# Delta rule: the inverse's first five levels on packed 32x32 diagonal blocks, the sixth as one off-diagonal block product

## The chip, the cores and the metric

The program runs on one core of one Trainium2 chip. The time is the device time of one execution in microseconds; the number given for a kernel is the median of its runs. The engines are named as in the profile: PE (TensorE, its weight loads apart as PEld), DVE (VectorE), ACT (ScalarE), POOL (GpSimd), SP (SyncE).

## What is computed

The whole program is a two-layer attention block followed by a second block with a gated delta rule and a Fourier mixer (512 positions, 256 of context, width 1024, 4 heads). The change touches one step of the second block, the inverse of a unit triangular matrix for each chunk of 64 positions, head and direction:

```python
CHUNK = 64
    lower = jnp.tril(jnp.ones((CHUNK, CHUNK), dtype=bool))
    strict = jnp.tril(jnp.ones((CHUNK, CHUNK), dtype=bool), -1)
...
    a_mat = jnp.where(strict, jnp.einsum('nbhid,nbhjd->nbhij', kb, kc) * decay, 0.0)
    eye = jnp.eye(CHUNK, dtype=f32)
    t_inv = lax.linalg.triangular_solve(eye + a_mat, jnp.broadcast_to(eye, a_mat.shape),
                                        left_side=True, lower=True, unit_diagonal=True)
    u_val = jnp.einsum('nbhij,nbhjd->nbhid', t_inv, vb)
    w_key = jnp.einsum('nbhij,nbhjd->nbhid', t_inv, kb * jnp.exp(gc)[..., None])
...
    def step(s, xs):
        u_i, w_i, a_i, qd_i, kd_i, gl_i = xs
        v_new = u_i - jnp.einsum('bhcd,bhde->bhce', w_i, s)
        o_i = jnp.einsum('bhcd,bhde->bhce', qd_i, s) + jnp.einsum('bhij,bhje->bhie', a_i, v_new)
        s = s * jnp.exp(gl_i)[..., None, None] + jnp.einsum('bhcd,bhce->bhde', kd_i, v_new)
```

Both directions are run: 12 chunks, 4 heads, 2 directions, 96 inverses of 64x64.

## The kernel before

The program is written out by hand, engine by engine: each engine has its own list of instructions and waits on semaphores, and nothing but those lists sets the order. Nearly all of the time PE multiplies 128x512 tiles of weights (the helper lines L977 to L979). The delta rule is a stretch of some 130 us late in the program.

The 96 inverses are made in three **groups** `g` (0, 1, 2). A group holds, for each direction `d`, two tiles of 128 positions (`j`), four heads (`h`) and the two chunks of a tile (`c`, partitions 0 to 63 and 64 to 127). One direction of a group is so one tile of 128 partitions x 512 columns, eight blocks of 64 columns, with two 64x64 matrices above each other in each. The inverse grows by doubling in six **levels**: at level `lev` the diagonal blocks of size 2^lev are known, and pairs of them are joined:

- POOL `mask` (L3562) writes `a_level`, the part of `a_mat` that couples the pairs.
- PE `level_z` (L1575) multiplies it by `tt_mat`, the inverse so far, transposed: 16 matmuls of 64x64 by 64x64 for a direction, those of `c` = 0 on one quarter of the array and those of `c` = 1 on the opposite one. Each is float32 and stands in the trace as two records, with two of a weight load; so 32 records for a direction, 64 for a pair of directions.
- ACT (L2239) copies the product out of PSUM into `z_mat`.
- PE `level_update` (L1587) multiplies by `t_mat`, again 16 matmuls for a direction.
- DVE `level_done` subtracts that from `tt_mat` (L3134) and turns it 32x32 block by block into `t_mat` (L3137).

Level 0 has no product: DVE takes the mask from the identity (L3124) and turns it (L3128). After level 5, POOL `gained` (L3596) and DVE (L3143) scale the inverse into `tt_gain` and `tt_beta`, and PE `w_and_u` multiplies keys (L1601) and values (L1617) by them.

In groups 1 and 2 the first four rounds of levels carry a step of the **scan** of the group before as well: on PE `scan_read` (L1637, and L1647 where an output is wanted) stands between `level_z` and `level_update`, `scan_write` (L1662, L1673) behind it; DVE subtracts into `u_rows` (L3157) ahead of its level work and adds to `state` (L3174) behind it; ACT decays the state (L2228). Behind each round PE has one or two Fourier products (`position_products`, L1461 and L1445). In group 0 POOL scales decay matrices between its masks, two tiles a level (L3571, L3581), and PE has `turn_x` (L1560) behind levels 4 and 5.

## Time and profile before

| | us |
|---|---|
| median of 3 runs | 2865.8 (2864.92 to 2869.05) |
| the profiled execution | 2867.95 |
| its span, first to last instruction | 2866.2 |
| PE busy in the span | 2819.9 (98%) |
| delta rule levels, first to last product | 2265.6 to 2385.6 |
| records of L1575 and of L1587 | 960 and 960 |

The profile is one execution. The 1.75 us between its time and its span lie around the program. The granted TensorE clock is full in all of the forty slices, also in those of the delta rule. Times in the trace count from the start of the span. A row of the chain of waits is one piece of the chain that ended last: start, duration, engine, tile written, line, number of records. In a row of the timeline what stands in brackets is the idle time of the engine before the group, and what ended it.

### The profile page before, as it was taken

What the parts mean: (1) busy time and instruction counts of PE and PEld (TensorE: products, weight loads), DVE (VectorE), ACT (ScalarE), POOL (GpSimd) and SP (SyncE); (2) the same over time, 40 slices, a digit from 0 to 9 for tenths busy, and PEclk for the clock granted to TensorE, in tenths of its full rate; (3) what the DMA queues carried; (4) which work ended last, traced back from release to release, by engine and by line L of the source; (5) the groups of instructions that cost most, each with busy time, mean ns of one, the idle gap of its engine ahead of it and who ended that gap; (6) DMA issues with size and microseconds to landing.
All of it is one profiled execution on the core that took longest, in us unless ns stands there. A gap on an engine that the chain in (4) does not pass through costs nothing.

```text
span 2866.2 us, 41070 instructions
## 1 busy us (share of the span) xinstructions
PE 2819.9 (98%) x16287; PEld 2271.5 (79%) x16287; DVE 1503.1 (52%) x2960; ACT 771.0 (27%) x1653; POOL 1595.4 (56%) x1116
## 2 busy tenths in 40 slices
PE   9999999999999999999999999999999998999998
PEld 5777778888888886777778888888878897788886
DVE  6663343247787126643542367884253566866601
ACT  5343332212211024343321122111032353311110
POOL 5444555667555564444556575556644554666664
PEclk9999999999999999999999999999999999999999
DMA  6434444445776554434445456775544101455553
GB/s 219 147 135 145 147 150 165 169 167 199 257 268 231 197 182 171 147 133 147 150 148 181 150 206 222 285 257 186 192 140 147 46 3 54 146 192 195 197 194 140
DMA packets 134065, 487.87 MB, mean 170 GB/s; under 512 B 15025, under 2 KB 16241, under 8 KB 133233
## 3 DMA queue, kind: packets, MB, share of 16 engines
q1 hardware_dynamic: 72096, 262.63, 27.6%
q0 software_dynamic: 60480, 220.23, 21.6%
q8 instruction: 130, 2.13, 0.3%
q10 hardware_dynamic: 1296, 2.37, 0.3%
q14 instruction: 63, 0.51, 0.1%
HBM read 483.04 MB, written 2.13 MB: 169 GB/s over the span
## 4 chain that ended last, share of the span: by engine, by line
PE 76%; issue 10%; POOL 9%; DVE 4%; ACT 1%; DMA 1%; SPq 0%; POOLq 0%; DVEq 0%; ACTq 0%
PE dense L977 20%; PE dense L979 20%; PE dense L978 20%; POOL raw_lo L3377 6%; PE scores L977 2%; PE scores L978 2%; PE scores L979 2%; POOL weights_hi L3363 1%; PE turned L1575 1%; PE turned L1587 1%; PE scores L1206 1%; PE O L1243 1%; POOL swapped_sin L3390 1%; PE turned L1231 1%; PE dense L1637 0%
## 5 line engine op out<-in xcount | busy, mean ns | idle before, releaser
L3377 POOL TENSOR_TENSOR raw_lo<-raw,weights_hi 128x1024 fp32r<-128x1024 f32 x420 | 1010.5, 2406 | 42.6 <-DMA weights_hi<-stream 31.5
L977 PE MATMUL dense<-h_hi,weights_hi 128*128 128x512 f32 x2096 | 833.4, 398 | 6.6 <-DVE gates L2475 2.2
L3363 POOL DMA_DIRECT2D weights_hi<-stream x420 | 243.1, 579 | 1055.1 <-PE dense L979 939.5
L979 PE MATMUL dense<-h_hi,raw_lo 128*128 128x512 f32 x2096 | 818.1, 390 | 0.0
L978 PE MATMUL dense<-h_lo,weights_hi 128*128 128x512 f32 x2096 | 817.3, 390 | 0.0
L977 PEld LDWEIGHTS dense<-h_hi,weights_hi 128*128 128x128 f32 x2096 | 394.0, 188 | 107.9 <-issue 16.0
L979 PEld LDWEIGHTS dense<-h_hi,raw_lo 128*128 128x128 f32 x2096 | 393.9, 188 | 84.7
L978 PEld LDWEIGHTS dense<-h_lo,weights_hi 128*128 128x128 f32 x2096 | 394.4, 188 | 76.8
L977 PE MATMUL dense<-hidden_hi,weights_hi 128*128 128x512 f32 x528 | 205.7, 390 | 1.4 <-POOL raw_lo L3377 1.4
L979 PE MATMUL dense<-hidden_hi,raw_lo 128*128 128x512 f32 x528 | 205.4, 389 | 0.0
L978 PE MATMUL dense<-hidden_lo,weights_hi 128*128 128x512 f32 x528 | 205.4, 389 | 0.0
L3336 DVE SCALAR_TENSOR_TENSOR side_b<-scores,small_sb,side_b 128x441 f32<-128x441 f32 (+2 forms) x176 | 122.3, 695 | 66.2 <-ACT side_b L2308 60.7
L2812 DVE SCALAR_TENSOR_TENSOR x<-dense,x 128x512 f32<-128x512 f32 x32 | 22.1, 691 | 223.7 <-PE dense L979 223.7
L2562 DVE TENSOR_TENSOR y_parts<-O,y_parts 128x512 fp32r<-128x512 f32 x24 | 16.6, 691 | 232.5 <-ACT y_parts L1934 232.5
L977 PEld LDWEIGHTS dense<-hidden_hi,weights_hi 128*128 128x128 f32 x528 | 99.1, 188 | 22.0 <-POOL raw_lo L3377 1.8
L979 PEld LDWEIGHTS dense<-hidden_hi,raw_lo 128*128 128x128 f32 x528 | 99.1, 188 | 20.8
L978 PEld LDWEIGHTS dense<-hidden_lo,weights_hi 128*128 128x128 f32 x528 | 99.1, 188 | 20.6
L1844 ACT ACTIVATE swapped<-dense 32x512 f32<-32x512 f32 x144 | 84.8, 589 | 88.7 <-PE dense L979 87.4
L1959 ACT ACTIVATE probs<-probs,neg_max 128x128 f32<-128x128 f32 (+3 forms) x128 | 71.0, 556 | 118.2 <-DVE neg_max L2607 118.2
L977 PE MATMUL dense<-y_parts,weights_hi 128*128 128x512 f32 x256 | 102.3, 400 | 0.0
L1944 ACT ACTIVATE probs_turned<-turned 128x128 f32<-128x128 f32 (+2 forms) x192 | 68.2, 408 | 119.8 <-PE turned L1231 119.4
L978 PE MATMUL dense<-y_parts,weights_hi 128*128 128x512 f32 x256 | 99.9, 390 | 0.0
(528 smaller groups left out, 4531.9 us busy)
## 6 DMA issues: line engine op xcount, KB each, us to landing
raw<-stream SPq DMA_DIRECT2D x425, 512.0 KB, 3.3
weights_hi<-stream POOLq DMA_DIRECT2D x420, 512.0 KB, 4.6
ada_w<-ada SPq DMA_DIRECT2D x48, 512.0 KB, 5.3
gates<-f_scratch SPq DMA_DIRECT2D x2, 1536.0 KB, 8.0
x<-x_in SPq DMA_DIRECT2D x4, 512.0 KB, 6.9
cond_rows<-cond SPq DMA_DIRECT2D x2, 1024.0 KB, 7.7
decays<-stream ACTq DMA_DIRECT2D x8, 193.5 KB, 4.4
out<-x SPq DMA_DIRECT2D x3, 512.0 KB, 2.7
```

Of the source, the lines that this page charges most:

```text
L977: nc.tensor.matmul(to, wh, xh, start=first, stop=False)
L978: nc.tensor.matmul(to, wh, xl, start=False, stop=False)
L979: return nc.tensor.matmul(to, wl, xh, start=False, stop=final)
L1206: last = nc.tensor.matmul(scores[:, hh, to], qT[c % 2][half, i * P:(i + 1) * P], keys[half, k0:k1], start=(i == s), stop=True, skip_group_ ...
L1231: last = nc.tensor.transpose(turned[:, hh, m * P:(m + 1) * P], prob(i, hh, SEQ)[:, m * P:(m + 1) * P], ident)
L1243: last = nc.tensor.matmul(O[half, m * P:m * P + n], values[:, m, v0:v0 + HEAD_DIM], probT(hh, m, n), start=(m == 0), stop=True, skip_group ...
L1844: last = nc.scalar.activation(swapped[32 * q:32 * q + 32, :], src[32 * (q ^ 1):32 * (q ^ 1) + 32, :], ACT.Copy)
L1944: last = nc.scalar.activation(probT_step(hh, i, k0 // P, k1 // P), turned[:, hh, 0:k1 - k0].rearrange("p (m n) -> p m n", n=P), ACT.Copy)
L1959: last = nc.scalar.activation(prob(s, hh, n), src, ACT.Exp, bias=neg_max[:, at:at + 1], scale=QK_SCALE if name == "D" else 1.0, accum_out= ...
L3336: nc.vector.scalar_tensor_tensor(out=u, in0=v, scalar=small[:, tap:tap + 1], in1=u, op0=ALU.mult, op1=ALU.add).then_inc(conv_step if m < 7 ...
L3363: nc.gpsimd.dma_start(w_hi(w), stream[DENSE.items[DENSE.weight_list[w]]]).then_inc(hi_landed[s], 16)
L3377: nc.gpsimd.tensor_tensor(lo, src, hi, ALU.subtract).then_inc(weights_lo, 1)
```

## The change

A constant `SUB` = 32 halves the chunk. Levels 0 to 4 only ever touch the two 32x32 blocks on the diagonal of a 64x64 matrix, and these are now held packed: tiles of 128 partitions x 256 columns (`a_level`, `t_sub`, `tt_sub`, `z_sub`), a block of 32 columns for each `j` and `h`, with the four diagonal blocks of two chunks above each other. Each multiplication of levels 1 to 4 is four matmuls of 32x32 by 32x32, on the four tiles on the diagonal of the array, in place of two of 64x64. Masks, copies, subtractions and turns of these levels work on 256 columns.

For POOL to read both diagonal blocks from the same columns, ACT first copies one of them into an empty off-diagonal place of `a_mat` (`pack_a`, two copies of 32 partitions for each direction; group 0's ahead of the levels, those of groups 1 and 2 behind the copies of levels 3 and 4 of group 0). POOL's first mask waits for that.

Level 5 needs no mask: the one off-diagonal block of the inverse is a product of the two diagonal ones with the block of `a_mat` between them. `last_z` and `last_update` are 16 matmuls of 32x32 for a direction each, two for each `j` and `h`. DVE spreads the two diagonal blocks into `tt_mat` (`diagonal_blocks`, 128 x 512 with a mask of zeros), and ACT writes the off-diagonal block from PSUM, negated (`last_blocks`, two copies of 32 partitions for each direction), in the place of DVE's last subtraction. What follows (`tt_gain`, `tt_beta`, `w_and_u`) is as before.

```diff
@@ PE
             def level_z(g, lev):
                 for d in range(2):
-                    pe.wait_ge(t_masked, level_no(g, lev, d))
+                    pe.wait_ge(t_masked, mask_no(g, lev, d))
                     pe.wait_ge(t_ready_g, level_no(g, lev - 1, d))
...
                     for j in range(2):
                         for h in range(GH):
+                            for q in range(4):
+                                rows, at = sub_part(q), sub_cols(j, h)
+                                last = nc.tensor.matmul(turned[rows, d, at], a_level[d][rows, at],
+                                                        tt_sub[d][rows, at], start=True, stop=True)
+                    last.then_inc(t_z, 1)
+
+            def last_z(g):
+                for d in range(2):
+                    pe.wait_ge(t_ready_g, level_no(g, LEVELS - 2, d))
+                    a = a_mat[mat_no(d, PAIR_GDN[d][g])]
+                    late, first = late_sub(d), 1 - late_sub(d)
...
                             for c in range(2):
-                                hs = half_rows(c)
-                                last = nc.tensor.matmul(turned[hs, d, c64(j, h)], a_level[d][hs, c64(j, h)],
-                                                        tt_mat[d][hs, c64(j, h)], start=True, stop=True)
+                                last = nc.tensor.matmul(turned[sub_in(c, first), d, sub_cols(j, h)],
+                                                        a[sub_in(c, late), first_cols],
+                                                        tt_sub[d][sub_in(c, late), sub_cols(j, h)], start=True, stop=True)
                     last.then_inc(t_z, 1)
@@ ACT
+            def pack_a(g):
+                for d in range(2):
+                    a = two_subs(a_mat[mat_no(d, PAIR_GDN[d][g])])
+                    late, first = late_sub(d), 1 - late_sub(d)
+                    act.wait_ge(a_ready, 2 * g + d + 1)
+                    for c in range(2):
+                        last = nc.scalar.activation(a[sub_in(c, first), :, late, :], a[sub_in(c, first), :, first, :], ACT.Copy)
+                    last.then_inc(a_packed, 1)
+
+            def last_blocks(g):
+                for d in range(2):
+                    late, first = late_sub(d), 1 - late_sub(d)
+                    act.wait_ge(t_upd, turn_no(g, LEVELS - 1, d))
+                    act.wait_ge(t_ready_g, level_no(g, LEVELS - 1, d))
+                    for c in range(2):
+                        rows = sub_in(c, first)
+                        last = nc.scalar.activation(two_subs(tt_mat[d])[rows, :, late, :],
+                                                    by_sub(turned[:, d, 0:2 * GH * SUB])[rows], ACT.Copy, scale=-1.0)
+                    last.then_inc(t_subbed, 1)
...
-                        nc.scalar.activation(z_mat[d], turned[:, d, :], ACT.Copy).then_inc(t_zc, 1)
+                        nc.scalar.activation(z_sub[d], turned[:, d, 0:2 * GH * SUB], ACT.Copy).then_inc(t_zc, 1)
+                    if g == 0 and lev in (3, 4):
+                        pack_a(lev - 2)
+                    if lev == LEVELS - 1:
+                        last_blocks(g)
@@ DVE
-                    nc.vector.tensor_tensor(tt_mat[d], tt_mat[d], turned[:, d, :], ALU.subtract).then_inc(t_subbed, 1)
-                    if lev < LEVELS - 1:
-                        dve.wait_ge(t_subbed, level_no(g, lev, d))
-                        nc.vector.transpose(t_mat[d], tt_mat[d]).then_inc(t_ready_g, 1)
+                    nc.vector.tensor_tensor(tt_sub[d], tt_sub[d], turned[:, d, 0:2 * GH * SUB], ALU.subtract
+                                            ).then_inc(t_subbed, 1)
+                    dve.wait_ge(t_subbed, level_no(g, lev, d))
+                    nc.vector.transpose(t_sub[d], tt_sub[d]).then_inc(t_ready_g, 1)
+
+            def diagonal_blocks(g):
+                for d in range(2):
+                    nc.vector.tensor_tensor(two_subs(tt_mat[d]),
+                                            by_sub(tt_sub[d]).unsqueeze(2).broadcast_to((P, 2 * GH, 2, SUB)),
+                                            sub_rows.rearrange("p (e n) -> p e n", e=2).unsqueeze(1
+                                                ).broadcast_to((P, 2 * GH, 2, SUB)), ALU.mult).then_inc(t_ready_g, 1)
@@ POOL
-                        pool.wait_ge(a_ready, 2 * g + d + 1)
+                        pool.wait_ge(a_packed, A_PACKED + 2 * g + d + 1)
...
-                    mask(g, lev)
+                    if lev < LEVELS - 1:
+                        mask(g, lev)
```

Order of the instructions on PE in group 0, before (a row is a run of equal instructions; x counts matmuls of the program, each two records in the trace; 64x64 is what one writes):

```order
L1575 MATMUL turned<-tt_mat,a_level 64x64 x32
L1587 MATMUL turned<-z_mat,t_mat 64x64 x32
L1461 MATMUL dense<-raw,p_0_160 128x256
L1560 MATMUL scores<-const,gdn_decay 64x64 x32
L1575 MATMUL turned<-tt_mat,a_level 64x64 x32
L1587 MATMUL turned<-z_mat,t_mat 64x64 x32
L1461 MATMUL dense<-raw,p_0_160 128x256
```

The same place after the change, levels 4 and 5:

```order
L1602 MATMUL turned<-tt_sub,a_level 32x32 x64
L1642 MATMUL turned<-z_sub,t_sub 32x32 x64
L1488 MATMUL dense<-raw,p_0_161 128x256
L1587 MATMUL scores<-const,gdn_decay 64x64 x32
L1616 MATMUL turned<-tt_sub,gdn_a 32x32 x32
L1630 MATMUL turned<-z_sub,t_sub 32x32 x32
L1488 MATMUL dense<-raw,p_0_161 128x256
```

Nothing has moved: level 4 has twice the matmuls, each a quarter of the size, level 5 has the same number. In groups 1 and 2 the lists change in the same two places of a round, and the scan's matmuls stand where they stood.

Order on ACT, from the last two Fourier copies ahead of the levels of group 0 to its end, before:

```order
L2156 ACTIVATE p_0_156<-dense 128x512
L2156 ACTIVATE p_0_160<-dense 128x512
L2239 ACTIVATE z_mat<-turned 128x512 x8
L2248 ACTIVATE gdn_decay<-scores 128x512 x2
L2239 ACTIVATE z_mat<-turned 128x512 x2
L2248 ACTIVATE gdn_decay<-O 128x512
```

And after:

```order
L2217 ACTIVATE p_0_157<-dense 128x512
L2217 ACTIVATE p_0_161<-dense 128x512
L2270 ACTIVATE gdn_a<-gdn_a 32x8x32 x4
L2324 ACTIVATE z_sub<-turned 128x256 x6
L2270 ACTIVATE gdn_a<-gdn_a 32x8x32 x4
L2324 ACTIVATE z_sub<-turned 128x256 x2
L2270 ACTIVATE gdn_a<-gdn_a 32x8x32 x4
L2337 ACTIVATE gdn_decay<-scores 128x512 x2
L2324 ACTIVATE z_sub<-turned 128x256 x2
L2281 ACTIVATE tt_mat<-turned 32x8x32 x4
L2337 ACTIVATE gdn_decay<-O 128x512
```

The copies of `pack_a` (L2270) have come in at three places, and those of `last_blocks` (L2281) behind the last copy of `z_sub`.

## Rows read from the trace of the kernel before

**Rows 1.** Busy time by stretch: groups 0, 1, 2 (x counts instructions).

```profile
core 0: us, PE busy (x) PEld busy (x) DVE busy (x) ACT busy (x) POOL busy (x), PEclk, DMA share, GB/s
2265.50:2301.10 35.60, 34.98 (x908) 32.27 (x908) 24.27 (x34) 13.42 (x23) 29.05 (x26) 1.00 0.01 3
2301.10:2345.50 44.40, 43.31 (x964) 39.39 (x960) 28.61 (x40) 23.34 (x56) 24.80 (x21) 1.00 0.01 3
2345.50:2394.20 48.70, 48.70 (x1024) 44.31 (x1024) 29.76 (x44) 26.14 (x69) 21.67 (x19) 1.00 0.01 3
```

**Rows 2.** Chain of waits, 2260 to 2396 us, shares by engine and line.

```profile
by line: PE turned L1575 19.6%; PE turned L1587 19.4%; PE dense L1461 7.2%; PE dense L1637 6.8%; POOL a_level L3562 6.7%; PE O L1662 6.1%; PE turned L1601 5.2%; PE dense L1673 3.0%; PE dense L1617 2.8%; PE turned L1617 2.6%; PE scores L1647
```

**Rows 3.** Chain of waits in order of time: one level of group 0.

```profile
2277.99 0.95 PE turned L1587 x32
2278.97 0.70 DVE tt_mat L3134
2279.69 0.71 DVE t_mat L3137
...
2281.86 1.15 PE turned L1575 x32
```

**Rows 4.** The same view: one round of group 1.

```profile
2309.36 2.01 PE turned L1575 x64
2311.37 1.02 PE dense L1637 x16
2312.40 2.01 PE turned L1587 x64
...
2316.56 2.01 PE turned L1575 x64
```

**Rows 5.** The same view: one round of group 2.

```profile
2354.66 2.01 PE turned L1575 x64
...
2357.69 0.87 PE scores L1647 x16
...
2363.75 2.01 PE turned L1575 x64
```

**Rows 6.** Lines L1575 and L1617: durations in ns, min/median/max.

```profile
L1575 PEld LDWEIGHTS turned<-tt_mat,a_level x960: 129/135/136, 2265.6 to 2383.7; 64*64 64x64 f32 x192
L1575 PE MATMUL turned<-tt_mat,a_level x960: 217/218/267, 2265.6 to 2383.7; 64*64 64x64 f32 x192
...
L1617 PE MATMUL dense<-vtok,tt_beta x96: 268/269/321, 2297.5 to 2392.2; 64*64 64x128 f32 x96
```

**Rows 7.** Chain of waits: two runs of records; timeline: the second one's shape.

```profile
2287.52 1.87 PE turned L1575 x64
2308.47 0.89 PE scores L1445 x8
2308.30 1.06 PE L1445 MATMUL scores<-fourier_sin,y_tail 128*128 128x128 f32 x8
```

**Rows 8.** Timeline, 2345.45 to 2345.53 us, PE and its weight loads.

```profile
2345.50 0.14 PEld L1575 LDWEIGHTS turned<-tt_mat,a_level 64*64 64x64 f32 x2 [0.21 <-POOL a_level L3562]
2345.50 0.27 PE L1575 MATMUL turned<-tt_mat,a_level 64*64 64x64 f32 x2
```

**Rows 9.** Groups of one shape: work on 256 columns (busy us, mean ns).

```profile
L3051 DVE TENSOR_TENSOR y_tail<-dense,y_tail 128x256 f32<-128x256 f32 x4 | 1.7, 420 | 15.8 <-ACT y_tail L2137 15.8
L1944 ACT ACTIVATE probs_turned<-turned 128x256 f32<-128x256 f32 x80 | 26.3, 381 | 65.6 <-PE turned L1231 65.6
L3401 POOL TENSOR_TENSOR squares_sum<-squares_sum,squares 128x256 f32<-128x256 f32 x5 | 4.0, 808 | 1.0 <-ACT squares L1767 0.5
```

**Rows 10.** Timeline: the first product, POOL's other work of a level, DVE in the scan.

```profile
2265.58 2.37 PE L1575 MATMUL turned<-tt_mat,a_level 64*64 64x64 f32 x64 [1.34 <-POOL a_level L3562]
2271.16 2.05 POOL L3571 TENSOR_TENSOR gdn_a<-gdn_decay,const 128x512 f32<-128x512 f32 x2
2312.44 1.40 DVE L3157 TENSOR_TENSOR u_rows<-u_rows,dense 64x512 f32<-64x512 f32 x2 [2.69 <-PE dense L1637]
```

More of the change, by code:

```diff
@@ L43 @@
 LEVELS = 6
+SUB = CHUNK // 2
 GRID_W = 64
@@ L577, in build_program @@
         rowsum = a_mat
[L578 to L580 removed]
+        tt_mat, tt_beta, tt_gain = (rows_of(name, at, 2) for name, at in (
+            ("tt_mat", TT_AT), ("tt_beta", TTB_AT), ("tt_gain", TTG_AT)))
+        a_level, z_sub, t_sub, tt_sub = ([t[:, at:at + 2 * GH * SUB] for t in rows_of(name, slot, 2)] for name, slot, at in (
+            ("a_level", AL_AT, 0), ("z_sub", Z_AT, 0), ("t_sub", T_AT, 0), ("tt_sub", T_AT, 2 * GH * SUB)))
         wT, u_rows, kd = rows_of("wT", WT_AT, 4), rows_of("u_rows", U_AT, 4), rows_of("kd", KD_AT, 4)
@@ L1572, in level_z, with last_update @@
                         for h in range(GH):
+                            for q in range(4):
[8 more added lines that the diff above has]
+                    late, first = late_sub(d), 1 - late_sub(d)
+                    for j in range(2):
+                        for h in range(GH):
+                            first_cols = slice((j * GH + h) * CHUNK + SUB * first, (j * GH + h) * CHUNK + SUB * (first + 1))
                             for c in range(2):
-                                hs = half_rows(c)
-                                last = nc.tensor.matmul(turned[hs, d, c64(j, h)], a_level[d][hs, c64(j, h)],
-                                                        tt_mat[d][hs, c64(j, h)], start=True, stop=True)
+                                last = nc.tensor.matmul(turned[sub_in(c, first), d, sub_cols(j, h)],
+                                                        a[sub_in(c, late), first_cols],
+                                                        tt_sub[d][sub_in(c, late), sub_cols(j, h)], start=True, stop=True)
                     last.then_inc(t_z, 1)
+            def last_update(g):
+                for d in range(2):
+                    pe.wait_ge(t_zc, turn_no(g, LEVELS - 1, d))
+                    first = 1 - late_sub(d)
+                    for j in range(2):
+                        for h in range(GH):
+                            for c in range(2):
+                                rows, at = sub_in(c, first), sub_cols(j, h)
+                                last = nc.tensor.matmul(turned[rows, d, at], t_sub[d][rows, at], z_sub[d][rows, at],
+                                                        start=True, stop=True)
+                    last.then_inc(t_upd, 1)
             def level_update(g, lev):
@@ L1584, in level_update @@
                         for h in range(GH):
-                            for c in range(2):
-                                hs = half_rows(c)
-                                last = nc.tensor.matmul(turned[hs, d, c64(j, h)], t_mat[d][hs, c64(j, h)],
-                                                        z_mat[d][hs, c64(j, h)], start=True, stop=True)
+                            for q in range(4):
+                                rows, at = sub_part(q), sub_cols(j, h)
+                                last = nc.tensor.matmul(turned[rows, d, at], t_sub[d][rows, at],
+                                                        z_sub[d][rows, at], start=True, stop=True)
                     last.then_inc(t_upd, 1)
@@ L1691, in _ @@
                 for lev in range(1, LEVELS):
-                    level_z(g, lev)
+                    if lev < LEVELS - 1:
+                        level_z(g, lev)
+                    else:
+                        last_z(g)
                     if g and lev < LEVELS - 1:
                         scan_read(4 * (g - 1) + lev - 1)
-                    level_update(g, lev)
+                    if lev < LEVELS - 1:
+                        level_update(g, lev)
+                    else:
+                        last_update(g)
                     if g and lev < LEVELS - 1:
@@ L3198, in _ @@
                         new_values(4 * (g - 1) + lev - 1)
-                    level_done(g, lev)
+                    if lev < LEVELS - 1:
+                        level_done(g, lev)
+                    else:
+                        diagonal_blocks(g)
                     if g and lev < LEVELS - 1:
@@ L3812, in _consts2 @@
     lev = []
-    for s in (1 << n for n in range(LEVELS)):
+    for s in (1 << n for n in range(LEVELS - 1)):
         lev.append((i // (2 * s) == j // (2 * s)) & (i % (2 * s) >= s) & (j % (2 * s) < s))
-    twice = [np.concatenate([m[0:CHUNK, 0:CHUNK]] * 2) for m in lev + [m.T for m in lev]]
-    return np.concatenate([*upto, *upto_c, same, *barred, *twice, i % CHUNK == local], axis=1).astype(np.float32)
+    subs = [np.concatenate([m[0:SUB, 0:SUB]] * 4) for m in lev + [m.T for m in lev]]
+    in_sub = np.arange(SUB)[None, :]
+    return np.concatenate([*upto, *upto_c, same, *barred, *subs, i % SUB == in_sub, i // SUB % 2 == local // SUB],
+                          axis=1).astype(np.float32)
 def _consts():
```

47 lines of the change are left out of this document (32 added, 15 removed).

## The prediction, made before the changed kernel had run

> **What bounds the kernel now.** I read the stretches first: in the delta rule PE is busy for 34.98 of 35.60 us in group 0, 43.31 of 44.40 in group 1 and all 48.70 in group 2, at the full clock, with next to no DMA [rows 1]. The shares of the chain say what PE does there: L1575 and L1587, the two products of a level, are 39% of it, and POOL's masks 6.7% [rows 2]. The chain in order of time then shows two regimes. In groups 1 and 2 a round is nothing but PE: two pairs of products of 2.01 us each, the scan's matmuls and the Fourier products in the gaps between them; a round takes 7.20 us in group 1 (2309.36 to 2316.56) and 9.09 in group 2 [rows 4, 5]. In group 0 there is no scan to fill PE, and the chain alternates: 0.95 us of L1587 for one direction, four DVE steps of about 0.7, 1.15 of L1575 for the other direction; from 2277.99 to 2283.01, 5.02 us a level [rows 3]. So the change is worth what it does to PE in eight rounds, and to PE, DVE and POOL together in group 0. What follows is again PE in its own order, so what is saved here should reach the end.
>
> **What one small record costs.** This is the term on which all rests. Today 64 records of L1575 take 1.87 us, 29 ns each; on the full array records of 128 columns follow each other in 0.89/8 = 111 ns [rows 7]. Half the columns on one array would be 56, so 29 means that two quarters work side by side, each at some 58 ns a record. The matmul record takes 218 ns at 64 moving columns and 269 at 128, so 0.8 ns a column [rows 6]. With 32 columns fewer I take 26 ns off and have 32 ns for one array. Four arrays side by side then give 8 ns a record. For that, instructions must start fast enough: after a wait two weight loads and two matmuls all start within the 10 ns of 2345.50 [rows 8], so 2.5 to 5 ns for each, and a record with its load needs no more than 8. The bounds are far apart: 8 ns if four arrays run as two do, 29 ns if records never come faster than the fastest of today [rows 7]. I take 8, since both rows of pace fit "time per array divided by arrays" and a 10 ns start is there to see. The number of records of a direction doubles from 32 to 64, so the break-even is at 14.6 ns; at 8 ns a direction takes 0.51 us in the place of 0.94, and a pair, with the change between directions, 1.05 in the place of 2.01.
>
> Today both halves of the array write the same tile `turned`, one direction of which is 512 float32 columns, and they overlap [rows 7]. The Trainium skill, "TensorEngine Tiling (Array Packing)", section "Restrictions and Gotchas", says that different row tiles can't access the same PSUM bank at once. By that rule 64 columns on two arrays would cost 56 ns a record, and the 29 ns of the row speak against it where the output partitions differ too, which holds for the four tiles of the change as well.
>
> **Part by part, from the profiled execution.**
> - *Rounds of group 1, four.* The two pairs give back 2 x (2.01 - 1.05) = 1.92 of 7.20. They covered something: between `scan_read` and `scan_write` DVE needs 1.40 us for `u_rows` [rows 10] and 0.1 to start, and `level_update` of 1.05 no longer covers it. Stall 0.45. Net 1.47 a round, 5.9 us.
> - *Rounds of group 2, four.* There L1647, 0.87 us [rows 5], stands in front of `level_update` too; 0.87 + 1.05 = 1.92 covers the 1.5. Net 1.92 a round, 7.7 us. DVE has room: 29.76 busy of 48.70 [rows 1].
> - *Group 0, levels 1 to 5.* DVE's four steps on 256 columns: 420 ns in the place of about 700 [rows 9, 3], for the turns I assume the same. The loop of PE and DVE falls from 5.02 to 0.51 + 1.65 + 0.51 and 0.2 of latencies, 2.9 us. POOL is then later: per level 2.05 us of scaling [rows 10] and two masks, 808 ns each by the nearest row of 256 columns [rows 9], 3.65 us. So three levels go from 5.02 to 3.65, 4.0 us; from level 4 to 5 POOL has no mask to deliver, and the halved products give 1.9. Together 5.9 us.
> - *The first product.* PE was idle for 1.34 us before it, waiting for the mask [rows 10]. `pack_a` puts two small ACT copies (381 ns by the nearest row [rows 9]) and a hop, 0.9 us, ahead of the first mask; three masks on the path give back 0.45 each, a subtraction 0.3, and the second direction overlaps. Nearly all the idle time goes, 1.2 us.
> - *The last level, three times.* 32 records a direction, as before, but of 32 columns on two arrays: 16 ns each, 0.51 us a direction; four of them in the place of 3.9 us give back 1.9. The end is new: instead of one DVE subtraction of 0.70 [rows 3] ACT makes two copies, 0.76 and a hop. After them POOL's first `tt_gain` (about 1.25 us) lets PE start L1601. That is 2.2 us behind the first half of `last_update`, and PE has 0.51 + 1.06 of its own to cover it in groups 1 and 2: stall 0.6. In group 0 the matmuls of L1560 cover it. So 1.9, 1.3 and 1.3; and of the 1.1 us in which PE was idle in group 1 [rows 1], nearly all of it at POOL's masks before group 2, 0.9 goes.
> - *At nothing:* `diagonal_blocks`, two DVE steps of some 0.7 us, lies beside `last_z` and its copies (1.5 us); if DVE were late there, it would cost up to 1.4 a group. The eight copies of `pack_a` for groups 1 and 2 stand behind ACT's copies of levels 3 and 4, 1.6 us each time; the next thing PE wants of ACT is the copy of the next level, over 2 us later. `z_sub`, 0.38 in the place of 0.60, is covered by the other direction or by the scan.
>
> Sum: 1.2 + 5.9 + 1.9 (group 0) + 5.9 + 1.3 + 0.9 (group 1) + 7.7 + 1.3 (group 2) = 26.1 us. From 2867.95 that is 2841.9; the median of the runs lies 2.15 us under the profiled one, so **2839.7**. With 10 ns a record instead of 8 it would be 2 to 4 us more; with no stall in the scan and none at the end, 3 us less; the small copies and turns are good for 3 either way. The likeliest case's own range is 2832 to 2848.
>
> **The rivals.**
> - *Half the arrays (0.17).* Four tiles side by side run no better than two pairs, each tile keeping its 58 ns: 14.6 ns a record. For it: no row shows more than two tiles at once. Against: 218 and 269 ns show that the time follows the columns [rows 6]. PE then gains nothing in levels 1 to 4; there remain the first product, 1.2, some 1.5 in group 0, where PE in order needs 4.6 us a level in the place of 5.02, and the last levels, 5.4. Sum 8.1: 2857.7 us.
> - *A record has a floor (0.20).* This is the one on the other side. If starting or feeding a record costs what the fastest one costs today, 29 ns, whatever its size, twice the records take twice the time: 3.74 us for a pair. The place is every product of levels 1 to 4, and the point from which it decides is 14.6 ns. The eight rounds of groups 1 and 2 grow by 2 x 1.73, 27.7 us; group 0 becomes PE-bound at 2 x 3.74 + 0.9 = 8.4 us a level, 13.5 us more over four; the last levels stay, the first product gives 1.2 back. +40: 2905.8 us. For it: nothing in the trace runs below 29 ns a record on average. Against: four instructions within 10 ns [rows 8], and 58 ns a quarter is what the columns explain by themselves. The Trainium skill, "TensorE: Matmul & The Clock Gate", section "Wait — 56ns, not 53.3ns?", states a floor from start to start of about 25 ns however few the columns, and "TensorEngine Tiling (Array Packing)", section "Performance Considerations", advises against taking a tiling factor from a dimension that is small already. By 25 ns a pair would be 3.2 us and the estimate some 25 us over the kernel before, near 2891. Since the starts of rows 8 are closer than that, I read the floor as one of a single tile.
> - *A wait takes the gain (0.03).* `last_blocks` or `pack_a` is far slower than priced. Ten small steps on the path would have to be off by a microsecond each.
>
> **How the numbers follow.** The forecast has 0.60, half the arrays 0.17, the floor 0.20, the wait 0.03. The range takes in the first two, with the low end for a pace under 8 ns and no stalls: 2830 to 2862, and leaves the floor out. A measurement of this kernel can tell about 0.2%, 5.7 us, from no change. Half the arrays, at 2857.7, lies just beyond that, so I count 0.10 of it as faster and 0.07 as the same. Faster 0.71, same 0.08, slower 0.21.
>
> **What the profile after would show.** Right: the 128-record groups of the products of levels 1 to 4 take about 1.05 us in the chain, a round of group 1 5.7 us and one of group 2 7.2; PE waits for `u_rows` by some 0.45 us in group 1; in group 0 masks stand in the chain, 3.6 us a level; DVE steps on 256 columns take 0.42 us. Half the arrays: the 128 records take 1.9 us. The floor: they take 3 us or more, PE is never idle in the levels and the rounds grow to 10 us and more. The forecast fails with the pace of the record; everything else in it is small change. If the pace is right and the time isn't, then the rounds were bound by the scan's own chain or by ACT, which the waits on `dense` L1637's successors would name.

## The result and the profile after

The changed kernel takes **2882.6 us**, the median of four runs (2877.0 to 2887.0), against 2866.7 (2864.9 to 2869.1) for the kernel before: a ratio of 1.0053, with a 95% interval of 1.0042 to 1.0065. It is slower by half a per cent, some 16 us, where 26 us of gain were forecast. The profiled execution is the shortest of the four: 2877.0 us, 9 us over the profiled one of before.

From the page of the kernel after, its instruction queue (packets, MB, share):

```profile
q8 instruction: 142, 2.33, 0.3%
```

The difference lies in the delta rule, 10.5 us in the profiled executions. Busy time by stretch, groups 0, 1 and 2 of the kernel after, inside the same work as [rows 1], and in the last line the stretch from the first product to the end of the values' products:

```profile
core 0: us, PE busy (x) PEld busy (x) DVE busy (x) ACT busy (x) POOL busy (x), PEclk, DMA share, GB/s
2264.30:2300.00 35.70, 26.38 (x1244) 21.82 (x1246) 13.46 (x27) 9.72 (x24) 13.55 (x17) 0.71 0.02 4
2308.00:2343.00 35.00, 29.30 (x1228) 24.85 (x1227) 17.09 (x33) 15.24 (x44) 7.05 (x9) 0.90 0.02 4
2355.00:2392.00 37.00, 32.19 (x1258) 28.17 (x1258) 21.98 (x40) 18.09 (x58) 6.31 (x8) 1.00 0.02 4
2264.30:2403.60 139.30, 117.30 (x4428) 102.28 (x4428) 67.39 (x118) 64.26 (x167) 53.27 (x59) 0.90 0.02 4
```

The kernel before had, from its first product to the same point:

```profile
2265.50:2394.30 128.80, 127.02 (x2892) 115.97 (x2892) 82.64 (x118) 62.91 (x148) 75.62 (x64) 1.00 0.01 3
```

PE's busy time did fall, from 127.0 to 117.3 us, although part of the stretch ran at a lower clock (0.90 on average, 0.71 in group 0). But PE is now idle for 22 of the 139.3 us, where it was idle for 1.8. Read the counts beside the times: PE issues a weight load and a matmul for each record, 8856 instructions instead of 5784. In groups 0, 1 and 2 that makes 2490, 2455 and 2516 instructions in 35.7, 35.0 and 37.0 us: 14.3, 14.3 and 14.7 ns an instruction, the same in three groups with different work and different company. Before, group 0 had 1816 in 35.60, 19.6 ns.

What ends the idle time is named by the longest waits of PE's weight loads in that stretch (us in total, times, longest), after:

```profile
PEld turned L1642 <- issue: 15.7, 19, 2.4
PEld turned L1602 <- issue: 7.0, 16, 0.9
```

"issue" is no engine: PE waited for nothing that the profile shows. PE's own matmuls of L1642 waited 13.3 us in total in the same way. Before, the longest of these waits for a level's products was 0.3 us. The chain of waits of group 0 after, in order of time, which answers [rows 3] (L1602 is the old L1575, L1642 the old L1587, L1587 the old L1560, L1488 the old L1461):

```profile
2264.37 1.42 PE turned L1602 x99
...
2266.96 2.30 issue
...
2274.27 1.91 issue
...
2276.49 1.95 PE dense L1488 x4
...
2292.89 3.61 PE scores L1587 x64
```

Every level now contains a hole, 2.30 and 1.91 us in the first two, in the middle of L1642. From 2264.37 to 2292.89 four levels take 7.13 us each; they took 5.02 [rows 3] and were to take 3.65. The second thing to see are the lines of dense work: four records of L1488 take 1.95 us, for which the next view has 1.06, and 64 of L1587 take 3.61, for which an experiment below has 2.01. These are the places where the granted clock is 0.50, that is 1.2 GHz instead of 2.4.

The same view of the rounds of group 1 and group 2, which answers [rows 4, 5]:

```profile
2308.93 0.68 PE turned L1602 x50
...
2317.28 1.41 PE turned L1602 x98
...
2324.05 0.24 PE turned L1602 x12
...
2335.67 1.86 PE turned L1602 x128
...
2342.62 0.65 PE turned L1616 x35
...
2354.34 0.68 PE turned L1602 x50
...
2378.23 2.29 issue
...
2382.70 1.06 PE dense L1488 x4
...
2391.87 0.65 PE turned L1616 x35
```

And in the kernel before, the first round of group 1 and the last levels of groups 1 and 2:

```profile
2301.25 2.00 PE turned L1575 x64
...
2330.96 2.01 PE turned L1575 x64
...
2381.94 2.01 PE turned L1575 x64
```

The first round of a group has two Fourier products behind it and is longer than the others, so like has to be compared with like. Before, the four rounds of group 1 took 8.11, 7.20, 7.20 and 7.20 us (2301.25 to 2330.96), 7.43 on average; now they take 8.35, 6.77, 11.62 and 6.95, 8.42 on average. Two of them are faster than before, and the whole loss is in the third, which has holes of 1.36 and 1.79 us and behind them a granted clock of 0.50. The four of group 2, from 2354.34 to the last level at 2391.87, take 9.38 each at the full clock and were 9.11 (2345.50 to 2381.94). And yet the products themselves are nearly as fast as forecast. The timeline has a whole pair at full clock:

```profile
2373.29 1.35 PE L1602 MATMUL turned<-tt_sub,a_level 32*32 32x32 f32 x128
```

128 records in 1.35 us, with the last one's own 0.19, leave 1.16 between the first start and the last: 9.1 ns from start to start. A record by itself, which answers [rows 6] (ns, min/median/max):

```profile
L1602 PE MATMUL turned<-tt_sub,a_level x1536: 183/192/258, 2264.4 to 2384.9; 32*32 32x32 f32 x192
```

192 ns instead of 218: the 26 ns that were taken off.

So four arrays do work side by side, and the time still went up. My **theory** for that: instructions reach PE at a limited rate. The instruction queue fetches blocks of 16 KB (2.33 MB in 142 packets), and by the counts a block holds 256 instructions: in the delta rule it fetched 34 packets after and 22 before, and 8856/256 = 34.6 and 5784/256 = 22.6:

```profile
q8 instruction: 34, 0.56, 1.6%
```

When a block is used up before the next is there, PE stands. A record of 9 ns asks for an instruction every 4.5 ns. **Rivals**: the records themselves stall when four tiles write one PSUM bank; the order of the four tiles exhausts something in the array; the new small steps of the last level or of `pack_a` disturb the rest; or the lower clock alone makes the loss.

### The profile page after: what moved, and what is told of

Read it like the earlier page. It is cut to its first block, busy times and chain, and to the rows that moved or that the text cites. A ratio compares the mean times of both kernels' runs of the same rounds, so it can differ in the third digit from the quotient of the medians.

```text
span 2875.2 us, 44154 instructions
## 1 busy us (share of the span) xinstructions
PE 2809.2 (98%) x17823; PEld 2256.5 (78%) x17823; DVE 1490.3 (52%) x2960; ACT 774.1 (27%) x1677; POOL 1572.4 (55%) x1110
## 3 DMA queue, kind: packets, MB, share of 16 engines
q8 instruction: 142, 2.33, 0.3%
## 4 chain that ended last, share of the span: by engine, by line
PE 75%; issue 11%; POOL 8%; DVE 4%; ACT 1%; DMA 1%; SPq 0%; POOLq 0%; DVEq 0%; ACTq 0%
PE dense L1004 20%; PE dense L1006 20%; PE dense L1005 20%; POOL raw_lo L3476 6%; PE scores L1004 2%; PE scores L1006 2%; PE scores L1005 2%; POOL weights_hi L3462 1%; PE scores L1233 1%; PE O L1270 1%; POOL swapped_sin L3489 1%; PE turned L1602 1%; PE turned L1642 1%; PE turned L1258 1%; DMA weights_hi<-stream 1%
## 5 line engine op out<-in xcount | busy, mean ns | idle before, releaser
L1004 PE MATMUL dense<-y_parts,weights_hi 128*128 128x512 f32 x256 | 102.3, 400 | 0.0
L1006 PE MATMUL dense<-y_parts,raw_lo 128*128 128x512 f32 x256 | 99.9, 390 | 0.0
```

Source lines behind the costliest of these rows:

```text
L1004: nc.tensor.matmul(to, wh, xh, start=first, stop=False)
L1006: return nc.tensor.matmul(to, wl, xh, start=False, stop=final)
```

## The experiments

**The order of the tiles.** All the matmuls of the changed kernel, but tiles 0 and 1 of every block first, and then 2 and 3, in both products (`level_update` likewise):

```diff
-                    for j in range(2):
-                        for h in range(GH):
-                            for q in range(4):
-                                rows, at = sub_part(q), sub_cols(j, h)
+                    for q0 in (0, 2):
+                        for j in range(2):
+                            for h in range(GH):
+                                for q in (q0, q0 + 1):
+                                    rows, at = sub_part(q), sub_cols(j, h)
```

> The changed kernel with its own matmuls of levels 1 to 4 in another order: first all those of array tiles 0 and 1, then those of tiles 2 and 3, so that two tiles run side by side in the place of four. Result and number of instructions are the same. Theory of the supply: the array would need 16 ns a record, which is still faster than instructions come, so the time is that of the changed kernel within 4 us, with the same gaps after every 256 instructions. Rival (four tiles collide): gaps go, the time moves by more than 8 us. If the forecast of 8 ns for four tiles and 16 for two holds, the runs between gaps last about twice as long.

Measured: 2884.2 us (2883.6 to 2887.1, four runs), 1.0059 (1.0045 to 1.0072) of the kernel before: no other time than the changed kernel's. The first stretch of group 0, by the columns of the view by stretch, and the hole that ends it, in the chain:

```profile
2263.80:2268.80 5.00, 3.46 (x249) 3.35 (x249) 0.87 (x2) 0.77 (x2) 5.00 (x7) 1.00 0.02 3
...
2267.28 1.51 issue
2268.79 0.34 PE turned L1644 x9
```

The records are slower: 249 of them keep PE busy for 3.46 us, 13.9 ns each, where 16 were expected for two tiles side by side; the changed kernel's first 247 kept it busy for 2.58 us, 10.4 each, and reached the hole after 2.59 us (2264.37 to 2266.96). So the runs between the holes lasted a third longer, not twice as long. What the slower records lose, the hole gives back: 1.51 instead of 2.30 us, and PE comes out of it at 2268.79, 4.97 us after its start at 2263.82, as it did in the changed kernel (2264.37 to 2269.26, 4.89 us). The end of the hole doesn't depend on how fast PE ran towards it. The order of the tiles is no cause.

**Half the instructions for the same stationary work.** In levels 1 to 4 one stationary block serves two neighbouring heads, with 64 moving columns: half the records, and the wrong factor for every second head. Everything else is the changed kernel:

```diff
-                        for h in range(GH):
+                        for h in range(0, GH, 2):
                             for q in range(4):
                                 rows, at = sub_part(q), sub_cols(j, h)
-                                last = nc.tensor.matmul(turned[rows, d, at], a_level[d][rows, at],
-                                                        tt_sub[d][rows, at], start=True, stop=True)
+                                two = slice(at.start, at.start + 2 * SUB)
+                                last = nc.tensor.matmul(turned[rows, d, two], a_level[d][rows, at],
+                                                        tt_sub[d][rows, two], start=True, stop=True)
```

> The changed kernel, in which one stationary block of 32x32 serves two neighbouring heads in levels 1 to 4 (64 moving columns, half the matmuls; every second head gets the wrong factor, so this leaves out half of the multiplications' own weights). Four array tiles, packed tiles, masks, copies and waits all stay; PE gets as many instructions as in the kernel before. Theory of the supply: the idle time ended by issue in the levels falls from about 30 us to under 3, the clock stays full, and the time is near the forecast, 2835 to 2845 us. Rival (four tiles at once, or the waits added on ACT, cost the time): it stays above 2870.

Measured: 2847.2 us (2840.6 to 2851.6, four runs), 0.9926 (0.9908 to 0.9943). The whole delta rule, by the same columns as above:

```profile
2261.90:2370.30 108.40, 100.72 (x2892) 87.24 (x2892) 66.34 (x118) 64.26 (x167) 52.95 (x58) 1.00 0.02 4
```

Its chain: L1587 at full clock, the starts of two rounds of group 1 and of two of group 2:

```profile
2278.04 2.01 PE scores L1587 x64
...
2299.56 1.03 PE turned L1603 x64
...
2305.34 1.03 PE turned L1603 x64
...
2344.18 1.03 PE turned L1603 x64
...
2351.43 1.03 PE turned L1603 x64
```

108.4 us in the place of 139.3, with the same tiles, the same PSUM tile, nearly the same DVE, ACT and POOL work and the same last level. The clock is 1.00 throughout, and 5784 instructions in 108.4 us are 18.7 ns each. This is the kernel that the prediction described: a pair in 1.03 us (forecast 1.05), a round of 5.78 in group 1 (5.73) and 7.25 in group 2 (7.17). Four tiles on one bank, `pack_a` and the last level are cleared as causes of the loss. Two things missed what was expected: the time is 2.2 us over the upper end, and the weight loads still wait at "issue" for 5.0 us in L1644 and 3.0 in L1603 (15.7 and 7.0 in the changed kernel), where under 3 together were expected. The holes that remain are where the demand is highest, in group 0:

```profile
2276.00 0.88 issue
```

By itself this run can't tell the count of instructions from the pause between short matmuls, since both were changed. The next three do.

**The burst by itself.** In the kernel before, 512 matmuls of 32x32 blocks over four tiles stand ahead of the first level. Each is a matmul in float32 and makes two records, so 1024 records and 2048 instructions; nothing on another engine is waited for or changed, and the results are overwritten:

```diff
             position_products(0, 0, BEFORE_LEVELS)
+            for i in range(512):
+                rows, at = slice(32 * (i % 4), 32 * (i % 4 + 1)), slice(32 * (i // 4 % 16), 32 * (i // 4 % 16 + 1))
+                nc.tensor.matmul(turned[rows, i // 256, at], ident[rows, 0:32], ident[rows, 0:32], start=True, stop=True)
```

> The kernel before with 512 float32 matmuls of 32x32 on four array tiles (identity by identity, into a tile that nobody reads then) put ahead of the first product of the levels: 2048 instructions in one run with no wait. Theory of the supply: at about 13.7 ns an instruction they take 26 to 29 us, in runs of 256 instructions with idle gaps ended by issue between them; the kernel is 24 to 30 us slower. Rival (instructions are supplied faster, the gaps come from the waits between levels): 8 to 10 us, no gaps.

Measured: 2898.9 us in one run, against 2867.1 of before beside it, 31.8 us more and 1.8 over the upper end of what was expected. The timeline of PE:

```profile
2265.75 1.29 PE L1692 MATMUL turned<-const 32*32 32x32 f32 x128 [0.51 <-issue]
2269.49 1.93 PE L1692 MATMUL turned<-const 32*32 32x32 f32 x128 [2.46 <-issue]
2272.97 1.93 PE L1692 MATMUL turned<-const 32*32 32x32 f32 x128 [1.54 <-issue]
2276.44 1.93 PE L1692 MATMUL turned<-const 32*32 32x32 f32 x128 [1.54 <-issue]
```

This is the cleanest picture of the cause. PE runs 128 records, 256 instructions, stands still, and runs the next 256. From start to start it is 3.74, 3.48 and 3.47 us here. When the clock falls, the 128 records take 1.93 us instead of 1.29 and the hole shrinks from 2.46 to 1.54: the period stays. So the rate is set by the blocks: 256 instructions in 3.47 us at best, **13.6 ns an instruction**, 27 ns a record. Over all seven periods of the burst (2265.75 to 2291.42) the mean is 3.67 us, 14.3 ns an instruction, which is what groups 0 and 1 of the changed kernel show. The DMA row of the same stretch (2264 to 2290 us, 40 slices of 0.65 us) shows the blocks come in, one every five or six slices:

```profile
GB/s 0 0 0 0 25 0 0 0 0 0 25 0 0 0 0 25 0 0 0 0 25 0 0 0 0 0 25 0 0 0 0 0 25 0 0 0 0 0 25 0
```

The Trainium skill, "Advanced Engine Details and Errata", section "ISA Cache", describes an instruction cache with lines of 16 KB, 256 instructions; it gives the size as 32 KB, for TensorE as 128 KB, and says "Only 2 cache lines!". The trace agrees with the line: the holes come every 256 instructions. Of the two sizes it fits the two lines: PE ran 248 records here and 247 in the run above, nearly two blocks, before the first hole of more than 1 us; nothing shows the eight blocks of 128 KB. How fast a line is refilled that section doesn't state.

The clock is the second part of the price. By the granted clock PE ran at half speed, 1.2 GHz, right behind the first long hole and to the end of the burst:

```profile
2269.40:2291.50 22.10, 11.67 (x774) 10.87 (x776) 0.00 (x0) 0.00 (x0) 0.00 (x0) 0.50 0.02 4
...
2291.75 3.61 PE turned L1575 x64
```

(the first line is of the view by stretch, the second of the chain). The fall follows the holes and is not the rival cause: in the first long one, from 2267.10 to 2269.40, the granted clock was still 1.00. 64 records of L1575 take 1.87 us in the kernel before [rows 7]; the first 64 behind the burst take 3.61. The burst began at 2264.02, so it took 27.7 us, 1.3 of which filled PE's idle time in front of the first product [rows 10]; with the 1.7 us of the slow product PE is 28.1 us late. The rest of the 31.8 us is no more than single executions differ by: those of before lie between 2864.0 and 2872.1.

**The burst with half the instructions, twice.** The same 512 matmuls in bfloat16 (`ident_16`), one record each, 1024 instructions; and 256 matmuls of 64x64 blocks in float32, also 1024 instructions:

```diff
-                nc.tensor.matmul(turned[rows, i // 256, at], ident[rows, 0:32], ident[rows, 0:32], start=True, stop=True)
+                nc.tensor.matmul(turned[rows, i // 256, at], ident_16[rows, 0:32], ident_16[rows, 0:32], start=True, stop=True)
```

```diff
+            for i in range(256):
+                rows, at = slice(64 * (i % 2), 64 * (i % 2 + 1)), slice(64 * (i // 2 % 8), 64 * (i // 2 % 8 + 1))
+                nc.tensor.matmul(turned[rows, i // 128, at], ident[rows, 0:64], ident[rows, 0:64], start=True, stop=True)
```

> As burst32, but the 512 matmuls of 32x32 are bfloat16: one weight load and one matmul record each, 1024 instructions in the place of 2048. Theory of the supply (it counts instructions, not matmuls or bytes of data): half of burst32's time, 12 to 16 us, again with a gap after every 256 instructions; the kernel is 11 to 17 us slower than before. Rival (a fixed time per matmul or per array tile): as long as burst32 (about 30 us), or as short as the array allows (4 us or less).

> The kernel before with 256 float32 matmuls of 64x64 on two array tiles at the same place: 1024 instructions, each record at the 29 ns of the kernel before. Theory of the supply: the array needs 15.0 us and the supply about 14, so there are no gaps or hardly any, and the kernel is 13 to 15 us slower. It would show that the kernel before runs just inside the supply. Rival (gaps come from any long run of small matmuls): gaps of 1 us and more after each 256 instructions, over 18 us.

Measured: 2883.8 and 2877.6 us, one run each, against 2865.5: 18.2 and 12.1 us more, each about 1 us outside what was expected (11 to 17 and 13 to 15). The bursts themselves take 12.4 us (2262.66 to 2275.04) and 15.15. Timeline of the bfloat16 burst, and after it that of the 64x64 one:

```profile
2267.86 1.19 PE L1692 MATMUL turned<-masks 32*32 32x32 bf16 x128 [2.29 <-issue]
2271.33 1.22 PE L1692 MATMUL turned<-masks 32*32 32x32 bf16 x128 [2.29 <-issue]
```

```profile
2261.54 15.15 PE L1692 MATMUL turned<-const 64*64 64x64 f32 x512
```

The bfloat16 burst has another type and one pass instead of two, and the same period, 3.47 us for 128 records: the limit counts instructions, not passes, bytes of data or columns. The 64x64 burst needs 15.15/1024 = 14.8 ns an instruction by its own arithmetic, a little more than the 13.6 to 14.3 that it is given, and it has no hole at all. That is why the kernel before has no such holes: its densest lines, 29 ns a record [rows 7], are 14.6 ns an instruction and run just inside it.

**A middle dose.** Shared blocks, as above, in levels 1 and 3 only, where half the heads then have the wrong factors; levels 2 and 4 as in the changed kernel:

```diff
-                        for h in range(GH):
+                        n_heads = 1 + lev % 2
+                        for h in range(0, GH, n_heads):
```

> The changed kernel with one stationary block for two heads in levels 1 and 3 only; levels 2 and 4 have all their matmuls (the products of levels 1 and 3 leave out half of the factors). A middle dose of instructions: 520 in a round of group 2 and 460 in one of group 1 on average, in the place of 650 and 590. Theory of the supply, 13.7 ns an instruction: rounds of 7.2 us in group 2 and 6.3 in group 1, levels of 5.3 us in group 0; idle time ended by issue between that of the two whole doses (about 30 us in the changed kernel, about 9 with shared blocks everywhere); the time 2852 to 2862 us. Rival (a threshold: any four-tile level at full number stalls): 2868 and more.

Measured: 2865.5 us (2857.4 to 2871.1, ten runs), 0.9997 (0.9987 to 1.0007). It lies between the full dose (2882.6) and the least (2847.2), at 2865.5 where the middle of the two is 2864.9, and 3.5 us over the upper end of what I had expected. Its stretch:

```profile
2260.00:2394.70 134.70, 119.51 (x3668) 104.26 (x3664) 68.03 (x121) 63.83 (x167) 54.39 (x60) 0.87 0.03 8
```

The clock is what I had under-estimated: 0.87 on average, no better than with the full dose, although 17% fewer records were issued (3668 for 4428). In this profiled execution, the third longest of the ten, the stretch is only 4.6 us shorter than the changed kernel's. Holes of 0.6 to 2.3 us remain, nearly all in levels 2 and 4, and the clock falls behind some of them. How the loss splits between holes and clock I can't say from these runs: no kernel has all the holes without the fall. Group 2 of the changed kernel has holes of up to 2.29 us at a clock of 1.00, and its rounds are 0.27 us longer than before, where group 1, with its fall, has 0.99.

**The last level alone.** The kernel before, with level 5 alone done as in the change (`last_z`, `last_update`, `last_blocks` on the unpacked tiles, no mask for it); no more instructions on PE than before:

```diff
-                    level_z(g, lev)
+                    if lev < LEVELS - 1:
+                        level_z(g, lev)
+                    else:
+                        last_z(g)
...
-                    level_update(g, lev)
+                    if lev < LEVELS - 1:
+                        level_update(g, lev)
+                    else:
+                        last_update(g)
...
-                    mask(g, lev)
+                    if lev < LEVELS - 1:
+                        mask(g, lev)
```

> The kernel before with level 5 alone changed: one off-diagonal block product of 16 + 16 matmuls of 32x32 a direction, no mask for it, ACT writes the block; levels 0 to 4 as they were. It adds no instruction to PE. Theory (instructions come to PE at no more than 256 in about 3.5 us, and the change is slow because it asks for twice as many in levels 1 to 4): no new idle time ended by issue, 1 to 2 us saved a group, 2 to 5 us less than before. Rival (32x32 products are what is slow, whatever their number): last products as slow as those of levels 1 to 4 in the changed kernel, no gain or a loss.

Measured: 2866.3 us (2863.7 to 2871.7, eleven runs), 1.0002 (0.9993 to 1.0011): no change that can be measured, where I had expected 2 to 5 us of gain. In the profiled execution the stretch is 126.2 us instead of 128.8. The end of group 2 in its timeline shows where the rest is:

```profile
2375.78 1.11 PE L1613 MATMUL turned<-tt_mat,gdn_a 32*32 32x32 f32 x64
2376.95 1.11 PE L1627 MATMUL turned<-z_mat,t_mat 32*32 32x32 f32 x64
...
2380.13 0.32 PE L1653 MATMUL turned<-tt_gain,ktok 64*128 64x64 f32 x1 [1.01 <-POOL tt_gain L3669]
```

The two products take 2.2 us (forecast 2.0), where those of the last level of before take near 4 (2.01 from 2381.94 above, and 1.87). Behind them PE waits for `tt_gain` for 1.01 us at the ends of groups 1 and 2, where 0.6 was forecast. And the way from group 0 to group 1 is POOL's, as the chain shows:

```profile
2291.63 2.89 POOL kd L3662 x2
2294.52 2.47 POOL a_level L3635 x2
2297.04 1.15 PE turned L1600 x32
```

PE's first product of the next group waits for POOL's masks (`a_level`), and an earlier PE only waits longer. POOL is late without need, by its own timeline:

```profile
2286.17 3.00 POOL L3669 TENSOR_TENSOR tt_gain<-tt_mat,const 128x512 f32<-128x512 f32 x2 [8.12 <-ACT tt_mat L2266]
```

It stood idle for 8.12 us in front of `tt_gain`, while the masks, which need nothing of this group's end, stood behind it.

**The masks first.** So, in that kernel, the first masks of the next group go ahead of `tt_gain` on POOL, into the idle time:

```diff
-                gained(g)
                 if g + 1 < GROUPS:
                     mask(g + 1, 0)
+                gained(g)
```

> The kernel with the last level alone changed, and POOL writes the first masks of the next group ahead of tt_gain and not behind it (level 5 no longer reads a_level, so the tile is free then). POOL sat idle 8 to 19 us there, and its chain tt_gain, masks, kd, masks (3.0, 2.5, 2.9 and 2.5 us) is what the first product of groups 1 and 2 waits for; 2.5 us of it go. As many instructions on PE as in the kernel before. Theory (what is left on the path between the groups is POOL): the first product of groups 1 and 2 starts 1 to 2 us earlier each, 2 to 4 us less than with the last level alone, 2860 to 2864 us. Rival (PE's own order, the keys' and values' products, is what is late there): no more than 1 us.

Measured: 2863.1 us (2860.6 to 2868.6, eleven runs), against 2868.2 of before beside it: 0.9986 (0.9977 to 0.9995). PE goes from the values' products straight into the next group's first product, in the chain at both borders:

```profile
2296.10 1.75 PE turned L1669 x32
2297.85 2.00 PE turned L1600 x64
```

This leaves nothing of the reference out and is the one such version here that is faster than the kernel before, by 0.14% or some 4 us: a small gain, though its interval leaves out 1, and a small part of the 26 forecast. A version of the change whose products go through PE in a single pass, as those of the bfloat16 burst do, would halve the instructions of a level without sharing blocks; it was not tried, and what it does to the result is open.

## Why the prediction was wrong, point by point

- **The pace of a record: nearly right.** Forecast 8 ns from start to start and 1.05 us a pair; at full clock the 128 records of a pair are 9.1 ns apart, the pair is 1.35 us in the timeline, and a matmul record 192 ns. "Half the arrays" (14.6 ns) falls. So does the rival of a floor in the form I gave it, "starting or feeding a record costs what the fastest one costs": single records follow each other in 9. The Trainium skill, "TensorE: Matmul & The Clock Gate", section "Wait — 56ns, not 53.3ns?", gives 25 ns from start to start as the least; over four tiles the rows show 9.1, so that floor doesn't hold across tiles. Its price for a long run of records came near the truth all the same, by luck and for another reason: 27 ns is what a record costs *on average* once its two instructions have to be fetched. Its sum, 2905.8 us, did not: 2882.6 was measured, and the rounds grew by 0.99 and 0.27 us on average, not by 3.46.
- **The step that failed** is this one: "For that, instructions must start fast enough: after a wait two weight loads and two matmuls all start within the 10 ns". A burst of four instructions out of what was already fetched was read as a rate that holds for hundreds. [rows 8] shows how fast PE starts instructions that it has; nothing in it says how fast they come. In its place the burst showed 13.6 ns an instruction, so a pair of 128 records, 256 instructions, can't repeat faster than every 3.47 us, whatever the array does. For a level of group 0 with its 516 instructions that is 7.0 us, and 7.13 was measured; the forecast had 3.65. A round is saved only by what else PE does in it, few instructions that take long: hence 8.42 and 9.38 us on average, over the 7.43 and 9.11 of before, where the forecast took 1.47 and 1.92 off.
- **What the prediction didn't have at all: the clock.** It took the granted clock of 1.00 [rows 1] as given. Behind holes it fell to half, 0.71 on average in group 0 of the kernel after, and then the dense work pays too: 3.61 us for 2.01 in L1587, 1.95 for 1.06 in L1488.
- **The frame of the sum: right for the rounds and the first product.** With the instructions halved, rounds of 5.78 and 7.25 us for 5.73 and 7.17. In group 0 a level takes 4.0 us (2261.94 to 2278.04 for four) for 3.65, and its chain holds PE and its holes, not POOL's masks. The time, 2847.2, is 7.5 us over the forecast. The idle time before the first product is 0.24 us in the kernel after, of the 1.34 of before, as forecast. PE's wait for `u_rows` in group 1 is 2.6 us over four rounds, 0.65 each, where 0.45 was forecast:

```profile
PEld O L1719 <- DVE u_rows L3255: 2.6, 4, 0.7
```

- **The last level: mechanism right, size wrong.** 1.9, 1.3, 1.3 and 0.9 were forecast, 5.4 us together. Alone in the kernel before it shortened the stretch of the profile by 2.6 and gave nothing in the medians: 1.01 instead of 0.6 at each `tt_gain`, and the 0.9 at the border of groups was not there, as the masks still stood behind `tt_gain` on POOL. Only with the masks moved is the kernel faster; how much of that is the last level's, no run separates.
- **The chances.** The rivals were all about the array: its tiles, its floor. Each was weighed by how the fastest row came about, and none by what that row had in reserve elsewhere. A row of 29 ns a record has a double reading: the array's pace, 58 ns for each of two quarters, and 14.6 ns an instruction. The count of instructions was in the page and should have been a term of its own.

## What to carry to other kernels

Price a change that cuts matmuls smaller by its instruction count first: instructions, weight loads included, times what the densest long stretch of the trace shows for one, and compare that with the time of the stretch; here the limit was 13.6 ns, and a record under 27 ns on average is not to be had for more than a few hundred instructions. Few starts within some nanoseconds behind a wait say nothing of a rate; look for a run of more than 512 instructions, since nearly two blocks can be there already. And when PE's idle time ends at "issue" at even distances, spread the small matmuls among long ones, or use fewer and wider ones (the first was not tried here); behind such holes the granted clock can fall and the dense work around them pays too.

## What the runs showed of the hardware that I had not expected

- Instructions come to PE in blocks of 16 KB, 256 instructions, one in 3.47 us at best when PE waits for them (3.74 at times, 3.67 on average over the float32 burst): 13.6 ns an instruction at best, equal for float32 and bfloat16 and at both levels of the clock (3.47 us at 1.00 in the bfloat16 burst, at 0.50 in the float32 one).
- Four 32x32 tiles do run side by side and write the same columns of one PSUM tile, on different partitions: 9.1 ns from start to start in float32, (1.19 - 0.18)/127 = 8 ns in bfloat16, the 0.18 being an estimate from the float32 record's 0.19.
- With the order 0, 1, 0, 1 and so on in the place of 0, 1, 2, 3 a record takes 13.9 ns of busy time instead of 10.4: how far tiles overlap depends on their order in the program.
- In the float32 burst the granted clock fell from 1.00 to 0.50 behind holes of 0.51 and 2.46 us and stayed there to its end, with PE busy for 11.67 of 22.10 us. A hole alone doesn't do it: behind the 2.29 us at 2378.23 in group 2 of the changed kernel L1488 still took 1.06 us, at 1.00.
